# Sixteen experts of a two-layer network: gate/up and down products of fourteen of them as seven quadrant products

## The chip, the cores and the metric

One Trainium2 chip, one of its NeuronCores. The metric is the device time of one execution in microseconds; times of several executions are compared by their median. All arithmetic is float32.

## What is computed

The reference is a network of two layers over 2048 rows of 1024 values. The change touches one part only, the experts at the end of the first layer. Each of 16 experts picks 256 rows (its capacity), and those rows go through a gated feed-forward block with 512 hidden values:

```
def expert_choice_ffn(h, w_router, w_gate, w_up, w_down):
    cap = CAPACITY * N // N_EXPERTS                      # 256 rows
    aff = softmax(h @ w_router)
    gate, idx = top_k(swapaxes(aff, 1, 2), cap)
    xg = h[idx]                                          # 256 x 1024 for each expert
    g = einsum('becd,edf->becf', xg, w_gate)             # 1024 x 512
    u = einsum('becd,edf->becf', xg, w_up)               # 1024 x 512
    y = einsum('becf,efd->becd', silu(g) * u, w_down) * gate
    return zeros_like(h).at[idx].add(y)
```

Everything else (the two mixers, the router, the second layer with its 32 experts) is the same in both kernels.

## The kernel before

The program is a sequence of stages with a barrier between them. The stage `moe1`, the function `experts`, is called once with 16 units. For each expert it does the following.

- SyncE (`sp`) loads the expert's gate, up and down weights (2 MB each) into one of two buffers each. The load of gate and up for expert e+2 waits until the gate/up products of e are made, that of down until its down products are. Behind the last load, `next_columns.load` fills the weight buffer of the next stage's projection (6 MB).
- GpSimd (`pool`) gathers the 256 rows of expert e+2 with two indirect DMAs, and adds the finished rows of e into the target with two more.
- TensorE (`pe`) transposes the gathered rows of the next expert (`turn`, L2981), 16 transposes for each expert in four groups of four, between the gate/up products of this one. Those products (L2999) are four blocks `f` of 128 hidden values; each is 8 matmuls with gate weights and 8 with up weights, a 128x128 weight tile held still and all 256 rows moving. The down products (L3016) are 4 banks of 4 matmuls, 512 output columns moving.
- ScalarE (`act`) copies the transposed rows out with scale and shift (`evacuate`, L3030) and takes Silu of the gate half (L3040).
- VectorE (`dve`) multiplies by the up half (L3057) and, behind the down products, multiplies by the row's gate and the modulation row into `y` (L3070). `gc` (L3054) is a copy of the rows' gates.

In the profile one float32 matmul of the program is two MATMUL records and two LDWEIGHTS records; a transpose is one of each. So an expert's gate/up products are 64 matmuls and 128 records, its down products 16 matmuls and 32 records. PSUM is two banks `psG`, two banks `psT` and four banks `psD`. The experts 0, 1, 14 and 15 are written out; the other twelve run in a loop of six turns.

Of the kernel before, what the change touches and what calls it, by code (L numbers as in the profile page):

```python
# [14 lines left out]
P = 128  # L15
# [2814 lines left out]
def experts(nc, name, K, units, J, FF, x_rows, table, wg, wu, wd, scale2, shift2, n_gates, gate_row, target, block_expert, next_columns,  # L2830
            shared):
# [7 lines left out]
    scatter = block_expert is None  # L2839
    assert FB == 2 * J  # L2840
    WB = 2 if scatter else 4
    TURNS = units // WB
    with Stage(nc, name) as s:
        g_rest = s.sb("g_w", [P, WB - 1, KD, FF])
        u_all = s.sb("u_w", [P, WB, KD, FF])
        g_w = [shared.weights_of(KD, FF)] + [g_rest[:, j, :, :] for j in range(WB - 1)]
        u_w = [u_all[:, j, :, :] for j in range(WB)]
        d_w = s.sb("d_w", [P, WB, FB, D])
        xg = [shared.tile, s.sb("xg", [P, J, D + n_gates])]
        xT = s.sb("xT", [P, 2, KD, N])  # L2850
        sg = s.sb("sg", [P, 2, N])
# [6 lines left out]
        psG = s.ps("psG", [P, 2, BANK])  # L2858
        psT = s.ps("psT", [P, 2, BANK])
        psD = s.ps("psD", [P, 4, BANK])  # L2860
        up_landed = [s.sem(f"up_landed{j}") for j in range(WB)]
        down_landed = [s.sem(f"down_landed{j}") for j in range(WB)]
# [3 lines left out]
        names = ("fixed", "at_ready", "at_out_ready", "gc_ready", "turned", "xT_ready", "made", "silued", "mixed",  # L2866
                 "lowered", "y_ready", "passed")
        (fixed, at_ready, at_out_ready, gc_ready, turned, xT_ready, made, silued, mixed,
         lowered, y_ready, passed) = (s.sem(n) for n in names)
        block = s.block()  # L2870
        STORES = 16 * (J if scatter else 1)
        halves_behind = ((), (0,), (1,), (2, 3))

        def half(i, j):

            return i * (WB // 2) + j // 2

        def turns(engine, body):

            for j in range(WB):  # L2880
                body(0, j, 2)
            with engine.Fori(1, TURNS - 1) as i:
                for j in range(WB):
                    body(i, j, 2)
            for j in range(WB):
                body(TURNS - 1, j, min(2, WB - 1 - j))

        def after(i, j, n):

            return (i, j + n) if j + n < WB else (i + 1, j + n - WB)  # L2890

        def early(i, j):

            return isinstance(i, int) and i == 0 and j < 2

        @block.sync
        def _(sp):
            def load(i, j, first):
                u = i * WB + j
                if scatter:  # L2900
                    e = u
                else:
                    e = sp.value_load(block_expert[0:1, bass.ds(u, 1)], min_val=0, max_val=wg.shape[0] - 1)
                if not first:
                    sp.wait_ge(made, (u - WB + 1) * FB)
                if first and j == 0:
                    sp.sem_inc(up_landed[j], 16)
                    for half, landed in enumerate((first_up, up_landed[j])):
                        c = slice(half * FF // 2, (half + 1) * FF // 2)
                        sp.dma_start(u_w[j][:, :, c], wu[bass.ds(e, 1), :, c].rearrange("e (k p) n -> p (e k) n", p=P)).then_inc(landed, 16)  # L2910
                else:
                    for buf, src in ((g_w, wg), (u_w, wu)):
                        sp.dma_start(buf[j], src[bass.ds(e, 1), :, :].rearrange("e (k p) n -> p (e k) n", p=P)).then_inc(up_landed[j], 16)
                if not first:
                    sp.wait_ge(lowered, (u - WB + 1) * 2 * J)
                sp.dma_start(d_w[:, j, :, :], wd[bass.ds(e, 1), :, :].rearrange("e (k p) n -> p (e k) n", p=P)
                             ).then_inc(down_landed[j], 16)
            for j in range(WB):
                load(0, j, True)
                if scatter and j == 0:  # L2920
                    sp.dma_start(gr[:, :], gate_row.to_broadcast([P, D])).then_inc(fixed, 16)
            with sp.Fori(1, TURNS) as i:
                for j in range(WB):
                    load(i, j, False)
            next_columns.load(sp)

        @block.gpsimd
        def _(pool):
            def gather(i, j):
                u, p = i * WB + j, j % 2  # L2930
                if not early(i, j):
                    pool.wait_ge(turned, (u - 1) * 2 * J)
                    if scatter:
                        pool.wait_ge(gc_ready, u - 1)
                pool.tensor_copy(at[:, p, :], table[:, bass.ds(u * J, J)]).then_inc(at_ready, 1)
                pool.wait_ge(at_ready, u)
# [6 lines left out]
            def put(i, j, left):  # L2943
                u, p = i * WB + j, j % 2
                if left == 2:
                    gather(*after(i, j, 2))
                if isinstance(u, int) and u == units - 1:
                    pool.drain()
# [22 lines left out]
        def _(pe):  # L2971
# [47 lines left out]
            for q in range(2 * J):  # L3019
                turn(0, 0, q)  # L3020
# [1710 lines left out]
```

## Time and profile before

| | |
|---|---|
| median of three executions | 4035.1 us (4034.43 to 4043.13) |
| profiled execution, its own time | 4038.21 us |
| its span | 4036.6 us |
| TensorE busy in the span | 3738.4 us (93%) |
| VectorE busy in the span | 2042.0 us (51%) |
| the experts' stage, first to last instruction | about 1554 to 2262 us |
| one expert in the middle of it | 43.5 us |

In all rows times are microseconds from the start of the span, unless they are marked ns or are a mean in ns. TensorE has two lines: PE for its matmuls, PEld for its weight loads, which run beside the matmuls. A busy time is a union: records that overlap count once. "Idle before" is the engine's idle time ahead of a group, with what ended it. PEclk is the granted TensorE clock as a share of full speed.

### The profile page before, as it was taken

Reading aid. Unit: us, or ns where it says so; the run is one execution under the profiler, and the core shown is the slowest. Engines: PE = TensorE matmul, PEld = TensorE weight load, DVE = VectorE, ACT = ScalarE, POOL = GpSimd, SP = SyncE. Lnnn points to the kernel's source line nnn. Section 1 sums busy time; section 2 is a strip of 40 time slices with the busy share of each in tenths; the row PEclk is TensorE's granted clock in tenths of the full one; section 3 lists DMA queues with packets and bytes.
Section 4 is the critical chain, followed back from the end, with each engine's and each line's share of the span. In section 5 each row is a group of like instructions: output and inputs, shape, how many; then the busy total and the mean of one; then the engine's idle time right before and its main releaser. Section 6 shows DMA issues by size and latency. Waiting matters only on the chain. (4 is left out here: it accounts for less than half of the span.)

```text
span 4036.6 us, 62344 instructions
## 1 busy us (share of the span) xinstructions
PE 3738.4 (93%) x21710; PEld 2426.7 (60%) x21728; DVE 2042.0 (51%) x4259; ACT 1538.0 (38%) x3417; POOL 645.8 (16%) x802
## 2 busy tenths in 40 slices
PE   6999999799898978999999799997999999599998
PEld 4667766555584435777777577774666655344444
DVE  1334343566597763111111278776333466678886
ACT  1122211355563422111111266764333223267775
POOL 0000000100173321111111001011000032322222
PEclk8999999899999988999999899998999999699999
DMA  6222112222435578556556212115222044498974
GB/s 242 78 77 83 71 68 88 88 72 82 129 112 192 182 258 311 183 185 210 187 177 211 70 48 63 59 54 149 68 67 77 23 141 141 167 330 271 333 240 102
DMA packets 227174, 574.09 MB, mean 142 GB/s; under 512 B 28154, under 2 KB 100986, under 8 KB 211118
## 3 DMA queue, kind: packets, MB, share of 16 engines
q1 hardware_dynamic: 177742, 395.92, 28.0%
q0 software_dynamic: 49248, 175.79, 14.9%
q8 instruction: 106, 1.74, 0.2%
q14 instruction: 78, 0.64, 0.1%
HBM read 433.59 MB, written 137.93 MB: 142 GB/s over the span
## 5 line engine op out<-in xcount | busy, mean ns | idle before, releaser
L884 PE MATMUL inp_psU<-inp_w,inp_hT 128*128 128x512 f32 (+3 forms) x1376 | 420.8, 464 | 0.0
L884 PEld LDWEIGHTS inp_psU<-inp_w,inp_hT 128*128 128x128 f32 x1376 | 256.1, 190 | 152.6 <-issue 122.4
L4519 DVE COPY moe_bu<-moe_wu 128x1024 f32 x480 | 299.0, 698 | 38.5 <-issue 19.5
L4406 PE MATMUL moe_psU<-moe_bu,shared_weights 128*32 128x256 f32 x3840 | 295.0, 382 | 1.9 <-issue 1.9
L4406 PE MATMUL moe_psU<-moe_wu,shared_weights 128*32 x1280 | 293.0, 382 | 1.4 <-DVE moe_bu L4519 1.0
L880 PE MATMUL inp_psU<-inp_hT,inp_w 128*128 128x256 f32 x1088 | 244.2, 385 | 9.4 <-DVE inp_tm L686 4.5
L3057 DVE TENSOR_TENSOR moe_hT<-moe_sg,moe_psG 128x256 f32<-128x256 f32 x64 | 27.0, 421 | 438.4 <-ACT moe_sg L3040 438.4
L3040 ACT ACTIVATE moe_sg<-moe_psG 128x256 f32<-128x256 f32 x64 | 24.5, 383 | 568.0 <-PE moe_psG L2999 568.0
L3735 PE MATMUL inp_psU<-shared_weights,inp_w 128*128 128x256 f32 x1024 | 232.3, 382 | 2.9 <-DMA inp_wg<-in_lru_wx 2.9
L880 PEld LDWEIGHTS inp_psU<-inp_hT,inp_w 128*128 128x128 f32 x1088 | 208.0, 193 | 41.5 <-issue 3.9
L2999 PE MATMUL moe_psG<-moe_xT,moe_u_w 128*128 128x256 f32 x1024 | 231.5, 379 | 0.0
L3016 PE MATMUL moe_psD<-moe_d_w,moe_hT 128*128 128x512 f32 x512 | 223.9, 595 | 3.3 <-DVE moe_hT L3057 2.3
L3735 PEld LDWEIGHTS inp_psU<-shared_weights,inp_w 128*128 128x128 f32 x1024 | 195.3, 192 | 36.0 <-issue 10.3
L2999 PEld LDWEIGHTS moe_psG<-moe_xT,moe_u_w 128*128 128x128 f32 x1024 | 194.6, 190 | 26.4
L4475 ACT ACTIVATE moe_bd<-moe_wd 128x1024 f32 x200 | 198.1, 1048 | 29.0 <-PE moe_psD L4428 29.0
L686 DVE COPY inp_tm<-inp_psU 128x512 f32<-128x512 f32 (+3 forms) x86 | 45.4, 527 | 316.0 <-PE inp_psU L884 316.0
L4406 PEld LDWEIGHTS moe_psU<-moe_wu,shared_weights 128*32 128x32 f32 x1280 | 134.2, 110 | 110.9 <-issue 11.2
L3016 PEld LDWEIGHTS moe_psD<-moe_d_w,moe_hT 128*128 128x128 f32 x512 | 96.0, 190 | 122.0 <-issue 119.8
L1317 DVE TENSOR_SCALAR_CACHE_REDUCE att_junk<-att_psS,att_snk 128x640 f32<-128x640 f32 x128 | 108.1, 882 | 108.6 <-PE att_psS L1236 108.6
L4428 PE MATMUL moe_psD<-moe_bd,moe_hT 128*32 128x512 f32 x960 | 153.0, 595 | 0.0
L4406 PEld LDWEIGHTS moe_psU<-moe_bu,shared_weights 128*32 128x32 f32 x3840 | 150.8, 110 | 2.9 <-issue 2.9
L4428 PE MATMUL moe_psD<-moe_wd,moe_hT 128*32 x320 | 151.1, 595 | 1.1 <-ACT moe_hT L4472 0.5
(737 smaller groups left out, 7336.2 us busy)
## 6 DMA issues: line engine op xcount, KB each, us to landing
moe_wu<-in_w_up SPq DMA_DIRECT2D x32, 2048.0 KB, 8.9
moe_d_w<-in_w_down SPq DMA_DIRECT2D x16, 2048.0 KB, 10.6
moe_wd<-in_w_down SPq DMA_DIRECT2D x32, 1024.0 KB, 10.8
moe_u_w<-in_w_up SPq DMA_DIRECT2D x15, 2048.0 KB, 13.4
mod_w<-in_w_ada SPq DMA_DIRECT2D x24, 1024.0 KB, 11.6
inp_mod_w<-in_w_mod SPq DMA_DIRECT2D x16, 1024.0 KB, 5.0
xn<-out_xn POOLq DMA_DIRECT2D x32, 512.0 KB, 4.8
shared_weights<-in_w_gate SPq DMA_DIRECT2D x8, 2048.0 KB, 8.5
```

The lines of the kernel that those rows point to most:

```text
L686: dve.tensor_copy(tm[:, j, at:at + n], psU[:, u % NB, 0:n]).then_inc(tm_kept, by)
L880: mm = pe.matmul(psU[:, u % NB, 0:G], w[:, k, fm_lo + u * P:fm_lo + (u + 1) * P], hT[:, par, k, :], start=(k == 0), stop=(k == KD - 1))
L884: mm = pe.matmul(psU[:, u % NB, 0:n], hT[:, par, k, j * P:(j + 1) * P], w[:, k, lo:lo + n], start=(k == 0), stop=(k == KD - 1))
L1317: dve.tensor_scalar(junk[:, kv, :], psS[:, kv, LO:LO + KEYS], 1.0, snk[:, 1, h:h + 1], ALU.mult, ALU.min, accum_out=low[:, j, h:h + 1]).th ...
L2999: mm = pe.matmul(psG[:, f % 2, at_col:at_col + N], w[j][:, k, f * P:(f + 1) * P], xT[:, p, k, :], start=(k == 0), stop=(k == KD - 1))
L3016: mm = pe.matmul(psD[:, b, :], hT[:, f, r * P:(r + 1) * P], d_w[:, j, f, h * BANK:(h + 1) * BANK], start=(f == 0), stop=(f == FB - 1))
L3057: dve.tensor_tensor(hT[:, f, :], sg[:, f % 2, :], psG[:, f % 2, N:2 * N], ALU.mult).then_inc(mixed, 1)
L3735: mm = pe.matmul(psU[:, m % 2, u % 2 * G:(u % 2 + 1) * G], w[:, k, TM2_W + u * P:TM2_W + (u + 1) * P], hT[:, par, k, :], start=(k == 0), s ...
L4406: mm = pe.matmul(psU[c, f, 0:2 * P], xT[:, p, k, c], w, start=(k == 0), stop=(k == KD - 1), tile_position=(0, g * LOT))
L4428: mm = pe.matmul(psD[c, n, :], hT[:, f, c], w, start=(f == 0), stop=(f == FB - 1), tile_position=(0, g * LOT))
L4475: return act.activation(bd[:, g - 1, f, :].unsqueeze(1), wd[:, bass.ds(slot, 1), f, :], ACT.Copy)
L4519: ins = dve.tensor_copy(bu[:, g - 1, f, c, :].rearrange("p k n -> p (k n)").unsqueeze(1), wu[:, bass.ds(slots[g - 1], 1), f, c, :].rearran ...
```

## The change

Gate and up of an expert are taken as one matrix of two by two quadrants (gate or up; first or second half of the 1024 inputs), the gathered rows as another (input half; first or second 128 rows). The product of two such matrices has eight quadrant products; the new `up` makes seven, on sums of quadrants (`ws1`, `ws2`, `ws4` and `up_of(e, 0)` overwritten on the weights' side; `xt1`, `xt2` and two quadrants of `xT` overwritten on the rows' side), and VectorE joins them with seven additions. `down` does the same with `hT` (`hs1`, `hs2`, `hs4`) and the down weights (`dt1`, `dt2`). A quadrant product of `up` is 16 matmuls with 128 rows moving, one of `down` is 2 matmuls with 512 columns moving. Each product has one of six PSUM banks in turn; `room` waits until the bank's last reader is through. Products run in the order P1, P2, P6, P5, P3, P7, P4. P1 is copied out by ScalarE (`keep`).

The experts 0 and 15 stay as they were (`plain_up`, `plain_down`). The sums, the joined results `U` and `V` and one gate buffer lie in `next_columns.w`, the next projection's weight buffer, whose load now waits until all products of expert 14 are made. The loops are gone: all 16 experts are written out. `make_w_left(e, n)` makes sum n of the weights' side (n = 1, 2, 4: a quadrant sum of 128 x 2048 into `ws1`, `ws2`, `ws4`; n = 3 overwrites `up_of(e, 0)`), `make_x_right` and `make_d_right` likewise on 128 x 512 and 128 x 1024; only the first branch of one of them is shown. Lines with "+" are new.

```
+        lent = next_columns.w[:, :, :].rearrange("p k n -> p (k n)")
+        taken_of_lent = [0]
+        def borrow(a, n):
+            lo = taken_of_lent[0]
+            taken_of_lent[0] = lo + a * n
+            return lent[:, lo:lo + a * n].rearrange("p (a n) -> p a n", a=a)
+        ws1, ws2, ws4 = (borrow(KH, FF) for _ in range(3))
+        xt1, xt2 = (borrow(KH, P) for _ in range(2))
+        dt1, dt2 = (borrow(FH, BANK) for _ in range(2))
+        hs1, hs2, hs4 = (borrow(FH, P) for _ in range(3))
+        U, V, sg_second = (borrow(1, BANK)[:, 0, :] for _ in range(3))
+        gates = [sg[:, :], sg_second]
+        ps = s.ps("ps", [P, BANKS, BANK])
-        psD = s.ps("psD", [P, 4, BANK])
...
+                    if e >= 2:
+                        sp.wait_ge(made, base(e - 2) + (FB if plain(e - 2) else 7))
+                    for buf, src in ((g_w[j], wg), (u_w[:, j, :, :], wu)):
+                        sp.dma_start(buf, src[e:e + 1, :, :].rearrange("e (k p) n -> p (e k) n", p=P)).then_inc(up_landed[j], 16)
+                if e >= 2:
+                    sp.wait_ge(made, base(e - 1))
+                sp.dma_start(d_w[:, j, :, :], wd[e:e + 1, :, :].rearrange("e (k p) n -> p (e k) n", p=P)).then_inc(down_landed[j], 16)
...
+            sp.wait_ge(made, base(LAST))
...
+            def room(n):
+                if n >= BANKS:
+                    reader, count = readers[n - BANKS]
+                    pe.wait_ge(joined if reader == "joined" else kept, count)
...
+            def up_product(e, i, w, x):
+                n = base(e) + i
+                room(n)
+                for f in range(FB):
+                    for k in range(KH):
+                        mm = pe.matmul(bank(n)[:, f * P:(f + 1) * P], w[:, k, f * P:(f + 1) * P], x[:, k, :],
+                                       start=(k == 0), stop=(k == KH - 1))
+                mm.then_inc(made, 1)
+            def up(e):
+                pe.wait_ge(up_landed[e % 2], 32 * (e // 2 + 1))
+                pe.wait_ge(xT_ready, 4 * e + 4)
+                up_product(e, P1, gate_of(e, 0), x_of(e, 0, 0))
+                up_product(e, P2, gate_of(e, 1), x_of(e, 1, 0))
+                turn(e + 1, 0)
+                pe.wait_ge(w_left, 4 * (e - 1) + 2)
+                pe.wait_ge(x_right, 4 * (e - 1) + 2)
+                up_product(e, P6, ws2, xt2)
+                turn(e + 1, 1)
+                up_product(e, P5, ws1, xt1)
+                turn(e + 1, 2)
+                pe.wait_ge(w_left, 4 * (e - 1) + 3)
+                up_product(e, P3, ws4, x_of(e, 1, 1))
+                turn(e + 1, 3)
+                pe.wait_ge(w_left, 4 * (e - 1) + 4)
+                pe.wait_ge(x_right, 4 * (e - 1) + 3)
+                up_product(e, P7, up_of(e, 0), x_of(e, 0, 1))
+                pe.wait_ge(x_right, 4 * (e - 1) + 4)
+                up_product(e, P4, up_of(e, 1), x_of(e, 1, 0))
+            def down_product(e, i, h, w):
+                n = base(e) + 7 + i
+                room(n)
+                for f in range(FH):
+                    mm = pe.matmul(bank(n), h[:, f, :], w[:, f, :], start=(f == 0), stop=(f == FH - 1))
+                mm.then_inc(made, 1)
+            def down(e):
+                pe.wait_ge(down_landed[e % 2], 16 * (e // 2 + 1))
+                pe.wait_ge(mixed, 2 * (e - 1) + 1)
+                down_product(e, P1, h_of(0, 1), d_of(e, 0, 0))
+                down_product(e, P2, h_of(1, 1), d_of(e, 1, 0))
+                pe.wait_ge(h_left, 4 * (e - 1) + 2)
+                pe.wait_ge(d_right, 4 * (e - 1) + 2)
+                down_product(e, P6, hs2, dt2)
+                down_product(e, P5, hs1, dt1)
+                pe.wait_ge(h_left, 4 * (e - 1) + 3)
+                down_product(e, P3, hs4, d_of(e, 1, 1))
+                pe.wait_ge(h_left, 4 * (e - 1) + 4)
+                pe.wait_ge(d_right, 4 * (e - 1) + 3)
+                down_product(e, P7, h_of(0, 0), d_of(e, 0, 1))
+                pe.wait_ge(d_right, 4 * (e - 1) + 4)
+                down_product(e, P4, h_of(1, 0), d_of(e, 1, 0))
+            for e in range(1, LAST):
+                up(e)
+                down(e)
+            plain_up(LAST)
+            plain_down(LAST)
...
+            def silu(e, n):
+                act.wait_ge(joined, joined_by(e, P3 if n else P2))
+                act.activation(gates[n], gates[n], ACT.Silu).then_inc(silued, 1)
+            def keep(e, down, to):
+                act.wait_ge(made, made_by(e, P1, down))
+                act.activation(to, bank(made_by(e, P1, down) - 1), ACT.Copy).then_inc(kept, 1)
+            for e in range(1, LAST):
+                if e > 1:
+                    act.wait_ge(mixed, 2 * (e - 1))
+                keep(e, False, U)
+                silu(e, 0)
+                for q in range(3):
+                    evacuate(e + 1, q)
+                silu(e, 1)
+                evacuate(e + 1, 3)
+                all_stored(act, e - 2)
+                keep(e, True, y_of(e, 0, 0))
...
+            def make_w_left(e, n):
+                if n == 1:
+                    dve.wait_ge(up_landed[e % 2], 32 * (e // 2 + 1))
+                    if e > 1:
+                        dve.wait_ge(made, made_by(e - 1, P5))
+                    ins = dve.tensor_tensor(ws1, up_of(e, 0), up_of(e, 1), ALU.add)
...
+            def make_h_left(e):
+                at_e = 4 * (e - 1)
+                dve.wait_ge(mixed, 2 * e)
+                dve.tensor_tensor(hs1, h_of(0, 0), h_of(1, 0), ALU.add).then_inc(h_left, 1)
+                dve.wait_ge(h_left, at_e + 1)
+                dve.tensor_tensor(hs2, hs1, h_of(0, 1), ALU.subtract).then_inc(h_left, 1)
+                dve.wait_ge(h_left, at_e + 2)
+                dve.tensor_tensor(hs4, h_of(1, 1), hs2, ALU.subtract).then_inc(h_left, 1)
+                dve.wait_ge(h_left, at_e + 3)
+                dve.tensor_tensor(h_of(0, 0), h_of(0, 1), h_of(0, 0), ALU.subtract).then_inc(h_left, 1)
+            def join(e, i, down, to, other, n):
+                dve.wait_ge(made, made_by(e, i, down))
+                if n:
+                    dve.wait_ge(joined, base(e) + 7 * down + n)
+                else:
+                    dve.wait_ge(kept, 2 * (e - 1) + down + 1)
+                dve.tensor_tensor(to, bank(made_by(e, i, down) - 1), other, ALU.add).then_inc(joined, 1)
+            def mix(e, r, up):
+                dve.wait_ge(silued, silued_before(e) + (2 if r else 1))
+                dve.wait_ge(joined, joined_by(e, P4) if r == 0 else joined_by(e, P7) - 1)
+                dve.tensor_tensor(hT[:, :, r * P:(r + 1) * P], tiles(gates[r]), tiles(up), ALU.mult).then_inc(mixed, 1)
+            def weigh(e, r):
+                dve.wait_ge(joined, joined_by(e, P4 if r == 0 else P3, True))
+                dve.scalar_tensor_tensor(out=y[:, e % 2, r, :], in0=y[:, e % 2, r, :], scalar=gc[:, e % 2, r:r + 1],
+                                         in1=gr[:, :], op0=ALU.mult, op1=ALU.mult).then_inc(y_ready, 1)
+            mix_plain(0)
+            make_w_left(1, 1)
+            make_w_left(1, 2)
+            make_x_right(1, 1)
+            make_x_right(1, 2)
+            weigh_plain(0)
+            make_w_left(1, 4)
+            make_w_left(1, 3)
+            make_x_right(1, 3)
+            for e in range(1, LAST):
+                keep_gates(e)
+                make_d_right(e, 1)
+                make_d_right(e, 2)
+                join(e, P2, False, gates[0], U, 0)
+                make_x_right(e, 4)
+                make_d_right(e, 3)
+                join(e, P6, False, U, U, 1)
+                join(e, P5, False, V, U, 2)
+                make_w_left(e + 1, 1)
+                join(e, P3, False, gates[1], V, 3)
+                make_w_left(e + 1, 2)
+                join(e, P7, False, V, V, 4)
+                join(e, P7, False, U, U, 5)
+                mix(e, 1, V)
+                make_x_right(e + 1, 1)
+                make_x_right(e + 1, 2)
+                join(e, P4, False, U, U, 6)
+                mix(e, 0, U)
+                make_h_left(e)
+                make_w_left(e + 1, 4)
+                all_stored(dve, e - 2)
+                join(e, P2, True, y_of(e, 1, 0), y_of(e, 0, 0), 0)
+                join(e, P6, True, y_of(e, 0, 0), y_of(e, 0, 0), 1)
+                make_d_right(e, 4)
+                join(e, P5, True, y_of(e, 0, 1), y_of(e, 0, 0), 2)
+                join(e, P3, True, y_of(e, 1, 1), y_of(e, 0, 1), 3)
+                weigh(e, 1)
+                join(e, P7, True, y_of(e, 0, 1), y_of(e, 0, 1), 4)
+                join(e, P7, True, y_of(e, 0, 0), y_of(e, 0, 0), 5)
+                join(e, P4, True, y_of(e, 0, 0), y_of(e, 0, 0), 6)
+                weigh(e, 0)
+                make_w_left(e + 1, 3)
+                make_x_right(e + 1, 3)
```

## Rows read from the trace of the kernel before

**Rows 1.** Busy time by stretch in the experts' stage, engine by engine, records as x.

```profile
core 0: us, PE busy (x) PEld busy (x) DVE busy (x) ACT busy (x) POOL busy (x), PEclk, DMA share, GB/s
1560.00:1610.00 50.00, 49.05 (x192) 36.71 (x193) 4.77 (x9) 8.19 (x23) 7.66 (x10) 0.95 0.94 339
...
1750.00:1850.00 100.00, 99.64 (x418) 75.43 (x417) 10.37 (x20) 18.65 (x50) 11.13 (x12) 1.00 0.52 168
```

**Rows 2.** Timeline, 1740 to 1790 us: start, duration, instruction, idle before.

```profile
1740.59 3.62 PE L2999 MATMUL moe_psG<-moe_xT,moe_u_w 128*128 128x256 f32 x16
...
1744.05 3.62 PE L2999 MATMUL moe_psG<-moe_xT,shared_weights 128*128 128x256 f32 x16
...
1766.91 14.00 PE L3016 MATMUL moe_psD<-moe_d_w,moe_hT 128*128 128x512 f32 x32 [0.23 <-DVE moe_hT L3057]
...
1780.74 3.62 PE L2999 MATMUL moe_psG<-moe_xT,moe_g_w 128*128 128x256 f32 x16
...
1780.94 0.75 DVE L3070 SCALAR_TENSOR_TENSOR moe_y<-moe_psD,moe_gc,moe_gr 128x512 f32<-128x512 f32 x1 [2.68 <-PE moe_psD L3016]
```

**Rows 3.** Timeline, 1795 to 1835 us.

```profile
1809.25 1.04 PE L2981 MATMUL moe_psT<-ident,shared_rows 128*128 128x128 f32 x8
...
1810.42 14.00 PE L3016 MATMUL moe_psD<-moe_d_w,moe_hT 128*128 128x512 f32 x32
...
1824.25 3.62 PE L2999 MATMUL moe_psG<-moe_xT,shared_weights 128*128 128x256 f32 x16
```

**Rows 4.** Timeline of TensorE in a later attention stage, 2930 to 2950 us.

```profile
2931.01 1.06 PE L3977 MATMUL lata_psO<-lata_v,lata_pT 128*128 128x128 f32 x8
2931.90 0.60 PE L3962 MATMUL lata_psP<-ident,lata_p_long 128*128 128x128 f32 x4
2932.34 1.06 PE L3977 MATMUL lata_psO<-lata_v,lata_pT 128*128 128x128 f32 x8
```

**Rows 5.** Groups by line and shape: TensorE, 128x128 and ahead of it the loads.

```profile
L3977 PE MATMUL lata_psO<-lata_v,lata_pT 128*128 128x128 f32 x544 | 74.6, 278 | 5.9 <-ACT lata_pT L4062 3.0 <-DVE lata_o L4023 2.9
...
L3977 PEld LDWEIGHTS lata_psO<-lata_v,lata_pT 128*128 128x128 f32 x544 | 67.9, 194 | 6.8 <-DVE lata_o L4023 3.4 <-issue 3.4
```

**Rows 6.** Groups by line and shape: VectorE.

```profile
L3070 DVE SCALAR_TENSOR_TENSOR moe_y<-moe_psD,moe_gc,moe_gr 128x512 f32<-128x512 f32 x64 | 48.1, 751 | 190.9 <-PE moe_psD L3016 190.9
...
L2214 DVE TENSOR_TENSOR out_xo<-out_psO,out_part 128x512 f32<-128x512 f32 x56 | 38.6, 689 | 75.3 <-PE out_psO L2393 62.2 <-DMA xn<-out_xn 12.3 <-DVE out_part L2242 0.5
...
L3351 DVE TENSOR_TENSOR inp_nope<-inp_qs,inp_hs 128x256 f32<-128x256 f32 x32 | 13.5, 422 | 1.3
...
L3388 DVE TENSOR_TENSOR inp_ig<-inp_ig,inp_xc 128x1024 f32<-128x1024 f32 x8 | 9.8, 1225 | 0.6
...
L2191 DVE TENSOR_TENSOR out_w<-out_w,shared_rows 128x2048 f32<-128x2048 f32 x2 | 4.5, 2288 | 3.0 <-DMA out_w<-in_w_out 3.0
```

**Rows 7.** One line of VectorE with its shortest, median and longest instruction (ns).

```profile
L2165 DVE TENSOR_TENSOR out_xo<-out_xo,out_x x14: 1224/1226/2068, 3267.6 to 3448.6; 128x1024 f32<-128x1024 f32 x14
```

**Rows 8.** Timeline, 1410 to 1425 us.

```profile
1410.69 0.69 DVE L2214 TENSOR_TENSOR out_xo<-out_psO,out_part 128x512 f32<-128x512 f32 x1 [1.78 <-PE out_psO L2393]
...
1411.41 1.39 DVE L2165 TENSOR_TENSOR out_xo<-out_xo,shared_rows 128x1024 f32<-128x1024 f32 x1
1411.80 2.15 POOL L2507 TENSOR_TENSOR out_left<-out_mixT,out_left 128x512 f32<-128x512 f32 x1
```

**Rows 9.** Groups by line and shape in the experts' stage: GpSimd.

```profile
L2961 POOL DMA_INDIRECT x<-moe_y,moe_at_out x32 | 51.0, 1595 | 590.6 <-DVE moe_y L3070 549.1 <-DVE moe_gc L3054 41.5
L2939 POOL DMA_INDIRECT moe_xg<-xn,moe_at x16 | 15.7, 982 | 9.1 <-POOL moe_at L2935 6.7 <-issue 2.4
```

**Rows 10.** DMA issues in the experts' stage: count, KB each, median us to landing.

```profile
moe_d_w<-in_w_down SPq DMA_DIRECT2D x16, 2048.0 KB, 10.6
moe_u_w<-in_w_up SPq DMA_DIRECT2D x15, 2048.0 KB, 13.4
...
inp_w<-in_w_in SPq DMA_DIRECT2D x2, 896.0 KB, 22.3
```

More of the change, by code:

```diff
@@ L2865, in experts @@
         stored = [s.sem(f"stored{j}") for j in range(2)]
[L2866 to L2869, printed above, removed]
+        names = ("fixed", "at_ready", "at_out_ready", "gc_ready", "turned", "xT_ready", "made", "silued", "joined", "kept", "mixed",
+                 "w_left", "x_right", "h_left", "d_right", "y_ready", "passed")
@@ L2870, in experts @@
+        (fixed, at_ready, at_out_ready, gc_ready, turned, xT_ready, made, silued, joined, kept, mixed,
+         w_left, x_right, h_left, d_right, y_ready, passed) = (s.sem(n) for n in names)
         block = s.block()
[L2871 to L2894, printed above, removed]
+        def silued_before(e):
+            return 0 if e == 0 else 4 + 2 * (e - 1)
+        def x_of(e, depth, r):
+            return xT[:, e % 2, depth * KH:(depth + 1) * KH, r * P:(r + 1) * P]
+        def h_of(depth, r):
+            return hT[:, depth * FH:(depth + 1) * FH, r * P:(r + 1) * P]
+        def d_of(e, depth, h):
+            return d_w[:, e % 2, depth * FH:(depth + 1) * FH, h * BANK:(h + 1) * BANK]
@@ L2896, in _ @@
         @block.sync
         def _(sp):
[L2898 to L2901, printed above, removed]
-                else:
[L2903 to L2917, printed above, removed]
@@ L2928, in _, with gather @@
         def _(pool):
[L2929 to L2936, printed above, removed]
+            def gather(e):
+                p = e % 2
+                if e >= 2:
+                    pool.wait_ge(turned, (e - 1) * 4)
+                    pool.wait_ge(gc_ready, e - 1)
+                pool.tensor_copy(at[:, p, :], table[:, e * J:(e + 1) * J]).then_inc(at_ready, 1)
+                pool.wait_ge(at_ready, e)
                 pool.sem_inc(passed, 1)
@@ L2964, in _ @@
             pool.wait_ge(first_up, 16)
-            gather(0, 1)
-            turns(pool, put)
+            gather(1)
+            for e in range(units):
+                put(e)
             for p in range(2):
@@ L2971, in _, with turn @@
         def _(pe):
-            def turn(i, j, q):
-                u, p = i * WB + j, j % 2
+            def turn(e, q):
+                if e > LAST:
+                    return
                 r, h = divmod(q, 2)
                 if q == 0:
-                    pe.wait_ge(gathered[p], half(i, j) * 16 * J + 16 * J)
-                if not (early(i, j) and j == 0 and r == 0):
-                    pe.wait_ge(xT_ready, u * 2 * J + q - 1)
+                    pe.wait_ge(gathered[e % 2], STORES * (e // 2 + 1))
+                if 4 * e + q >= 2:
+                    pe.wait_ge(xT_ready, 4 * e + q - 1)
@@ L3019, in _ @@
-            for q in range(2 * J):
-                turn(0, 0, q)
-            turns(pe, body)
+                        n = base(e) + FB + 2 * r + h
+                        room(n)
+                        for f in range(FB):
+                            mm = pe.matmul(bank(n), hT[:, f, r * P:(r + 1) * P], d_w[:, e % 2, f, h * BANK:(h + 1) * BANK],
+                                           start=(f == 0), stop=(f == FB - 1))
+                        mm.then_inc(made, 1)
[7 more added lines that the diff above has]
+                mm.then_inc(made, 1)
@@ L3036, in body @@
                 for f in range(FB):
-                    act.wait_ge(made, u * FB + f + 1)
-                    if not (early(i, j) and j == 0 and f < 2):
-                        act.wait_ge(mixed, u * FB + f - 1)
-                    act.activation(sg[:, f % 2, :], psG[:, f % 2, 0:N], ACT.Silu).then_inc(silued, 1)
-                    if left:
-                        for q in halves_behind[f]:
-                            evacuate(*after(i, j, 1), q)
-            for q in range(2 * J):
-                evacuate(0, 0, q)
@@ L3069, in body @@
[L3069 to L3075 removed]
+                        n = base(e) + FB + 2 * r + h
```

275 lines of the change are left out of this document (180 added, 95 removed).

## The prediction

> **What bounds the kernel now.** I read the busy time by stretch first. In the middle of the experts' stage TensorE is busy 99.64 of 100 us at full clock, VectorE 10.4, ScalarE 18.7, and the DMA engines about half [rows 1]. So the stage lasts as long as TensorE's queue, and only fewer or cheaper matmul records shorten it. The timelines give their price. Sixteen records of 256 columns run from 1740.59 to 1744.05, 216 ns each [rows 2]. The 14.00 us of a down block are 32 records of 512 columns, the last of which lasts about 0.6 us, so a step is 429 ns. Eight transposes and the turn to the down block take 1.17 us [rows 3]; I price 16 of them at 1.76 us, 110 ns each. One expert lasts from 1780.74 to 1824.25, 43.51 us [rows 2, 3]: 128 x 0.216 = 27.65, 32 x 0.429 = 13.73, 1.76, and 0.37 of small waits at the turns between the blocks.
>
> **TensorE's part of the change.** Each of 14 experts goes from 128 records of 256 columns to 7 x 16 matmuls, 224 records of 128 columns. The stage has no such stream, only transposes. The nearest is in a later attention stage, also float32, 128x128 weights, 128 columns, two records for each matmul: eight records and the start of the next group take 0.89 us, and those eight with four transposes go from 2931.01 to 2932.34, 1.33 us for twelve [rows 4]: 111 ns a step. That is the price I take. The group's row says 74.6 us for 544, or 137 ns [rows 5], but a union of runs of eight counts each run's last record in full (1.06 us for a step of 0.89) and the next group's start again. It is the upper bound. The lower bound is half of 216, 108 ns.
> Gate/up: 224 x 0.111 = 24.86 us in place of 27.65, so an eighth fewer columns saves a tenth. Down: 7 products of 4 records, 28 x 0.429 = 12.01 in place of 13.73. Transposes stay. The new expert is 24.86 + 12.01 + 1.76 = 38.63 us in place of 43.51, of which the 0.37 of turns vanishes only if no wait stands there. Saved: 4.88 us x 14 = 68 us.
>
> A rule speaks against this. The LDWEIGHTS of 128 columns last 194 ns each by the profile and overlap with the matmuls and one another, since the steps are 111 ns [rows 4, 5]. The Trainium skill (TensorE: Matmul & The Clock Gate, section Back-to-back issue gap) says that load and matmul together set the spacing, 81 ns at 128 columns where the formula for the isolated matmul gives 56; by that ratio of 1.45 the step here would be an estimated 155 ns and the expert 48.5 us. The trace's 111 ns decides against it, in runs of 12 records only.
>
> **VectorE's part.** It has 4 sums of 128x2048 at 2.29 us, 4 of 128x1024 at 1.225, 4 of 128x512 (xT) at 0.69, 4 of 128x256 at 0.42, 14 joins and 2 mixes of 512 at 0.69 [rows 6], 2 weighings of 1024 in SBUF (no row; between the 0.75 of 512 and twice that, so 1.27 by the growth of the sums), one copy of the gates at 0.16. That is 9.2 + 4.9 + 2.8 + 1.7 + 11.0 + 2.5 + 0.2 = 32.3, and 35 gaps of 0.03 [rows 8] make 33.4 us of 38.6. It fits, but the queue is in order, so I lay it beside TensorE's from t = 0 at the first up product (3.55 us a product, 0.44 four transposes, 1.72 a down product; results reach VectorE 0.20 us after the next matmul's start, 1780.94 against 1780.74 [rows 2], and I take the same back).
> Up P6 starts at 7.54, P5 at 11.5, P3 at 15.5, P7 at 19.5, P4 at 23.06; down starts at 26.6, its P6 at 30.0, P4 at 36.9.
> - P7's result is seen at 23.26. Two joins, mix, and two xT sums of the next expert end at 26.9; P4's result has just come (26.8). Join, mix, `hs1`, `hs2` end at 29.25, so TensorE may go at 29.45 where it needs them at 30.0. This is the tightest place, 0.6 us, and its cover is the two down products on rows whose mix is done (needed at 26.6, there at 25.4).
> - `hs4`, the h quadrant, `ws4` of the next expert, three joins and the last d sum end about 35.2, before 36.9.
> - Behind down P4 VectorE has a tail: joins to 40.1, weighing 41.4, weights and xT quadrants to 44.5, that is 5.9 us into the next expert, two d sums 8.4, then P2's join (made at 7.1). P7 wants those quadrants at 19.5. It has caught up by P6 at 11.3.
> - Banks: a product needs the reader of the sixth before it. The closest is down P7, needing up P4's join (27.6) at 35.2. Free.
> - ScalarE: about 8 us an expert before [rows 1] and two copies of 512 more. The evacuation that the third group of transposes needs at 15.1 stands behind P2's join (9) and one Silu; there is room.
> So I put a stall of 0.3 us an expert in the sum, 4 us in all, for the tight place; 0 is the lower bound.
>
> **Moved and removed.** The load of gate and up for e+2 is issued at 26.6 of e, and u lands 13.4 us later [rows 10], at 1.4 of e+1; VectorE first reads it at 15.3. Down weights issued at a start land at 10.6, read at 5.9 of the next. On SyncE's queue nothing else stands between them. Bytes: three weights of 2 MB, 1 MB gathered and 1 MB added, 8.4 MB an expert over 38.6 us, are 217 GB/s, under the 339 of the stage's first stretch [rows 1]. GpSimd keeps two gathers and two scatters; the gather for e+1 goes out some 7 us into e-1, so about 30 us early. The projection's 6 MB go out at the start of expert 15; they landed in at most 22.3 us [rows 10], under its 43 us. If that cover were gone it would cost those 22 us once. Expert 1's sums: its up weights are to be there before the sums are wanted at about 1593, since all 8.5 MB issued ahead fit in 25 to 30 us at 339 GB/s; VectorE then runs 0.5 us later than in steady state. Loops gone: the written-out experts 0 and 1 lie in the first stretch, where TensorE is busy 49.05 of 50 us with the DMA engines at 0.94 [rows 1], so written-out code costs nothing there, and the loop cost nothing to be gained.
>
> **The sum.** 4038.2 (the profiled execution) - 68 + 4 = 3974. The median is 3.1 us lower, 4035.1, so 3971.
>
> **Rivals.**
> - VectorE falls late, 20 in 100. For: 33.4 of 38.6 us with 0.6 us of room at one place; the two-input sum of 1024 has lasted 1.39 and up to 2.07 us, not 1.226, beside GpSimd's work [rows 7, 8]. GpSimd has two scatters and two gathers of 1.6 and 0.98 us an expert [rows 9], 5.2 us with 0.9 us of copies on top; if each held VectorE up, it would need 39.5 us, and as the queue is in order TensorE would wait 1 to 2.5 us an expert. Against: the scatters and gathers fall between 38 and 8 of the next, where there is slack. Time: 3967 + 14 to 35, 3981 to 4002.
>  The Trainium skill (SBUF — State Buffer, section Who interferes with whom) says that a tensor_tensor with both inputs in SBUF contends with GpSimd's reads and the later one blocks wholly; the 1.39 and 2.07 us agree, and whether an indirect DMA counts as such a read no row shows.
> - The 128-column step is 137 ns in trains of 32 (the group's row), slower, 5 in 100: 224 x 0.137 = 30.7, expert 44.5, 1.0 us x 14 more, 4049. It decides from a step of (43.51 - 13.77)/224 = 133 ns. Against: no idle is seen between the runs that give 111.
> - Loads don't overlap, 2 in 100: 224 x 0.194 = 43.5, expert 57.2, 13.7 x 14 more, 4227. The page's rule above goes this way, a third as far. The rows of 111 ns exclude nearly all of it.
> - Weights, instructions of the written-out code, or the projection's load come late, 4 in 100: some 20 to 50 us lost, 3990 to 4020.
> That the change doesn't make fewer columns is excluded; it is in the code.
>
> **Numbers.** Forecast 3971, 69 in 100, its own range 3962 to 3980. Half the time of the first rival is under 3992, so 3960 to 3994 holds about 8 in 10. A change of 0.2% (8 us) is about what can be told from none. Faster: 69 + 20 + 3 = 92; within 0.2%: 2; slower: 6.
>
> **What would show it.** In the changed profile: the up matmuls at 111 ns a step in trains of 32, 38.6 to 39 us an expert, VectorE about 85 busy of 100 us, TensorE over 97, and the first matmul of down P6 waiting 0 to 0.5 us on `hs2`. Wrong, if the step is 130 or more, if waits on `joined`, `w_left` or `x_right` stand before up P6 or P7, or if the next stage waits for its weights.

## The result, and the profile after

The changed kernel takes 3973.05 us (median of 4, 3966.75 to 3976.59), the kernel before in the same session 4039.11 (4034.43 to 4043.72): a ratio of 0.9835, interval 0.9815 to 0.9854. Beside each other once more on another chip they took 3968.44 and 4033.32, ratio 0.9837 [0.9823, 0.985]. Forecast were 3971 and a range of 3960 to 3994.

Busy time by stretch of the changed kernel; the two rows answer to [rows 1]:

```profile
1560.00:1610.00 50.00, 47.16 (x184) 35.46 (x184) 9.07 (x11) 13.13 (x36) 6.01 (x8) 0.87 0.92 338
1750.00:1850.00 100.00, 100.00 (x660) 79.91 (x659) 82.05 (x94) 19.07 (x47) 19.11 (x14) 1.00 0.68 219
```

TensorE doesn't idle in the middle of the stage. VectorE has gone from 10.37 to 82.05, the DMA engines from 168 to 219 GB/s, and neither stops it. The timeline from 1755 to 1800 us shows one whole expert, from down block to down block:

```profile
1756.13 3.60 PE L3092 MATMUL moe_ps<-moe_d_w,moe_hT 128*128 128x512 f32 x8
...
1758.31 0.42 DVE L3260 TENSOR_TENSOR inp_w<-inp_w,moe_hT 128x256 f32<-128x256 f32 x1
...
1759.57 3.60 PE L3092 MATMUL moe_ps<-inp_w 128*128 128x512 f32 x8
...
1767.94 1.61 POOL L2996 DMA_INDIRECT x<-moe_y,moe_at_out  x1 [27.47 <-DVE moe_y L3283]
...
1770.54 2.28 DVE L3210 TENSOR_TENSOR moe_u_w<-moe_g_w,moe_u_w 128x2048 f32<-128x2048 f32 x1
1771.46 2.82 POOL L2996 DMA_INDIRECT x<-moe_y,moe_at_out  x1 [1.91 <-DVE moe_y L3283]
...
1775.73 3.74 PE L3063 MATMUL moe_ps<-inp_w 128*128 128x128 f32 x32
...
1777.00 1.22 DVE L3249 TENSOR_TENSOR moe_d_w<-moe_d_w 128x1024 f32<-128x1024 f32 x1
...
1777.08 1.97 POOL L2974 DMA_INDIRECT moe_xg<-xn,moe_at  x1 [0.30 <-issue]
...
1779.30 0.60 PE L3018 MATMUL moe_psT<-ident,shared_rows 128*128 128x128 f32 x4
...
1783.51 0.69 DVE L3273 TENSOR_TENSOR inp_w<-moe_ps,inp_w 128x512 f32<-128x512 f32 x1 [3.32 <-PE moe_ps L3063]
...
1794.91 3.60 PE L3092 MATMUL moe_ps<-moe_d_w,moe_hT 128*128 128x512 f32 x8
1795.10 0.37 SPq L2954 DMA_DIRECT2D moe_g_w<-in_w_gate  x1
1795.11 0.69 DVE L3273 TENSOR_TENSOR inp_w<-moe_ps,inp_w 128x512 f32<-128x512 f32 x1 [0.16 <-PE moe_ps L3063]
```

- From 1756.13 to 1794.91 are 38.78 us, against 43.51 [rows 2, 3]: 4.73 us saved in each of 14 experts, 66.2 in all.
- A product of 32 records of 128 columns goes from 1775.73 to the transposes at 1779.30: 3.57 us, 111.6 ns a record in a long train, where [rows 4] gave 111 from trains of 12.
- `hs2` ends at 1758.73 and down P6, which reads it, starts at 1759.57 with no idle time in brackets: 0.84 us lie between them in the tight place.
- VectorE waits for TensorE, 3.32 us ahead of P5's join and 0.16 ahead of P4's.

The whole stage I measure from its first transpose to the first row load of the next stage. In before:

```profile
1553.93 1.94 PE L2981 MATMUL moe_psT<-ident,shared_rows 128*128 128x128 f32 x8 [6.86 <-PEq L76]
...
2268.01 0.82 SPq L3198 DMA_DIRECT2D shared_rows<-x  x2
```

and after:

```profile
1559.55 1.94 PE L3018 MATMUL moe_psT<-ident,shared_rows 128*128 128x128 f32 x8 [6.92 <-PEq L76]
...
2207.61 0.81 SPq L3454 DMA_DIRECT2D shared_rows<-x  x2
```

That is 714.1 and 648.1 us: 66.0 less, all of the gain and the 66.2 of the experts. Below, "the stage" is this measure. The spans differ by 62.0 only: this profile reached the stage 5.6 us later and was 1.6 us shorter behind it. The next projection's first matmul waits 2.47 us for a small load (`inp_wg`), so the 6 MB of its weights cost nothing.

### The profile page after: what moved, and what is told of

It reads as the page before. It is cut to its first block and busy times, and to the rows that moved or that the text cites. A ratio compares the mean times of both kernels' runs of the same rounds, so it can differ in the third digit from the quotient of the medians.

```text
span 3974.6 us, 65105 instructions
## 1 busy us (share of the span) xinstructions
PE 3673.2 (92%) x22998; PEld 2426.7 (61%) x23016; DVE 2407.5 (61%) x4623; ACT 1549.3 (39%) x3417; POOL 686.1 (17%) x802
## 5 line engine op out<-in xcount | busy, mean ns | idle before, releaser
L2996 POOL DMA_INDIRECT x<-moe_y,moe_at_out x32 | 68.3, 2136 | 482.0 <-DVE moe_y L3283 414.8
L1363 ACT ACTIVATE att_p<-att_psS,att_low 128x640 f32<-128x640 f32 x128 | 101.2, 792 | 119.3 <-DVE att_junk L1317 97.9
L4714 ACT ACTIVATE shared_weights<-moe_psT,mod_cols,mod_scale 128x128 f32<-128x128 f32 x320 | 120.1, 457 | 48.6 <-PE moe_psT L4650 48.6
L4318 ACT ACTIVATE lata_pT<-lata_psP 128x512 f32<-128x512 f32 (+3 forms) x112 | 61.1, 549 | 159.4 <-PE lata_psP L4218 159.4
L3129 ACT ACTIVATE moe_xT<-moe_psT,mod_cols,mod_scale 128x128 f32<-128x128 f32 x256 | 95.4, 456 | 70.7 <-PE moe_psT L3018 70.6
L3273 DVE TENSOR_TENSOR inp_w<-moe_ps,inp_w 128x512 f32<-128x512 f32 x84 | 58.1, 692 | 104.0 <-PE moe_ps L3063 102.6
```

The source lines that it names most:

```text
L1363: act.activation(p[:, g % 2, kv, :], psS[:, kv, LO:LO + KEYS], ACT.Exp, scale=-1.0, bias=low[:, j, h:h + 1], accum_out=sums[:, j, h:h + 1] ...
L2996: pool.indirect_dma_start(out=target, out_offset=bass.IndirectOffsetOnAxis(ap=at_out[:, p, r:r + 1], axis=0), in_=y[:, p, r, :], in_offset ...
L3129: ins = act.activation(xT[:, e % 2, k, r * P:(r + 1) * P], psT[:, h, (k % 4) * P:(k % 4 + 1) * P], ACT.Identity, scale=scale2[k], bias=shi ...
L4714: ins = act.activation(xT[:, p, k, :], psT[:, q, (k % 4) * P:(k % 4 + 1) * P], ACT.Identity, scale=scale2[k], bias=shift2[k])
```

## The experiments

The versions are made from the changed kernel, with two sets, `UP7` and `DOWN7`, that say which experts make their gate/up and their down products in seven. Ratios are to the kernel before, run on the same chip.

**The same program with nothing in seven products.** It keeps six PSUM banks, written-out experts and the later projection load.

```
-    def plain(e):
-        return e in (0, LAST)
+    UP7, DOWN7 = set(range(0)), set(range(0))
```

> All 16 experts make their products as before (64 and 16 matmuls), in the rewritten program: no loops, six PSUM banks in turn, load of the next projection's weights at the start of the last expert. Theory A (the gain is TensorE's fewer records alone): the time of the kernel before, 4039 us within 5, one expert 43.5 us, the stage from its first transpose to the next stage's first load 714 us. Theory B (a part of the gain comes from the rewrite: loops, banks, waits at the turn between blocks): 10 to 25 us below the kernel before, one expert 42 to 43 us.

Measured: 4035.16 against 4035.66, ratio 1.000 [0.9991, 1.001]; stage 713.0 us, an expert 43.44. So loops, banks and the place of the load are worth nothing, as predicted, and the whole gain is in the products.

**Each half alone.**

```
+    UP7, DOWN7 = set(range(1, 15)), set(range(0))  # up_only
+    UP7, DOWN7 = set(range(0)), set(range(1, 15))  # down_only
```

> Experts 1 to 14 make gate/up in seven quadrant products, down as before in 16 matmuls. Theory A: gate/up is 224 steps of 0.1116 us in place of 128 of 0.216, 25.0 in place of 27.65 us, so 2.65 us an expert and up to 0.37 more where the wait at the turn to the down products goes: 37 to 42 us below the kernel before, about 4000. Theory C (128-column products are worth nothing, the whole gain lies in the down products and the turns): within 5 us of the kernel before, one expert 43.5 us.

> Experts 1 to 14 make down in seven quadrant products, gate/up as before in 64 matmuls. Theory A: 28 steps of 0.429 us in place of 32, 1.72 us an expert, 24 us below the kernel before, about 4015; with the run of gate/up alone the two savings add up to the 66 us of both. Theory C: the whole 66 us less, about 3973.

TensorE's timeline, first with gate/up alone, then with down alone:

```profile
1757.95 13.90 PE L3093 MATMUL moe_ps<-moe_d_w,moe_hT 128*128 128x512 f32 x32
1771.69 7.31 PE L3102 MATMUL moe_ps<-moe_xT,moe_g_w 128*128 128x128 f32 x64
...
1798.44 13.90 PE L3093 MATMUL moe_ps<-moe_d_w,moe_hT 128*128 128x512 f32 x32
```

```profile
1766.08 3.67 PE L3134 MATMUL moe_ps<-moe_d_w,moe_hT 128*128 128x512 f32 x8
...
1778.17 3.62 PE L3076 MATMUL moe_ps<-moe_xT,moe_g_w 128*128 128x256 f32 x16
...
1807.82 3.67 PE L3134 MATMUL moe_ps<-moe_d_w,moe_hT 128*128 128x512 f32 x8
```

Gate/up alone: 3992.08, ratio 0.9892 [0.9876, 0.9909]; an expert takes 40.49 us, 3.02 less than [rows 2, 3], which is 27.65 - 25.00 = 2.65 and the 0.37 of waits at the turns. Down alone: 4010.87, ratio 0.9935 [0.9918, 0.9951]; an expert takes 41.74, 1.77 less (13.73 - 12.01 = 1.72). Together that is 4.79 us an expert beside 4.73 for both in one. The medians save 43.6 (37 to 42 were expected) and 24.8 us, together 68.4, beside 66.1. They add up but for 2 us, which is within what the rest of the program varies by (below); TensorE never waits for what either adds.

**How much room VectorE has, and where.** Two needless 128x1024 sums, 2.47 us an expert, are put in a place where VectorE waits anyway, and then into the tight chain.

```
                     join(e, P6, False, U, U, 1)
+                    (two sums)                      # extra_slack
                     join(e, P5, False, V, U, 2)
...
                     join(e, P7, False, U, U, 5)
+                    (the same two sums)             # extra_tight
                     mix(e, 1, V)
```

> The changed kernel with one of VectorE's sums (128x1024, 1.22 us) made twice more for each of 14 experts, in the place where VectorE has idled 3.3 us, between the joins of up products P6 and P5. Theory A (only the stretch from P7's result to the second h sum can hold TensorE up): no change, 3973 us within 5, one expert 38.8 us. Theory D (VectorE as a whole is at its limit, 82 of 100 us busy, and anything more falls on TensorE): 2.5 us an expert, 34 us more, about 4007.

> The same two extra sums (2 x 1.22 us) placed between the joins of up product P7 and the first mix. Theory A: in the changed kernel the second h sum ends 0.84 us before the first matmul that reads it, of which about 0.2 is the way between the engines; so of 2.5 us more some 1.9 fall on TensorE, one expert 40.7 us, 26 us more, about 3999. Theory D: the same 34 us as in the other place. Theory E (the room is larger than it looks, since the end of P4's join and not P7's starts the chain): under 10 us more.

The stretch from 1750 to 1850 us with the sums in the slack, then in the tight chain:

```profile
1750.00:1850.00 100.00, 100.00 (x660) 79.91 (x660) 87.95 (x101) 18.74 (x45) 23.04 (x17) 1.00 0.72 234
```

```profile
1750.00:1850.00 100.00, 96.49 (x617) 75.08 (x616) 83.80 (x97) 17.43 (x42) 16.76 (x13) 1.00 0.65 211
```

In the slack they cost nothing: 3969.66, ratio 0.9839 [0.9823, 0.9856], stage 647.5, with VectorE the busier for it. In the chain: 3987.95, ratio 0.9891 [0.9874, 0.9907], stage 670.3, so 18.3 us by the medians and 22.9 by the stage where 26 were expected. The timeline of the latter shows which waits:

```profile
1796.63 3.67 PE L3135 MATMUL moe_ps<-moe_d_w,moe_hT 128*128 128x512 f32 x8 [1.17 <-issue]
...
1799.75 0.42 DVE L3310 TENSOR_TENSOR inp_w<-inp_w,moe_hT 128x256 f32<-128x256 f32 x1
...
1800.23 3.70 PE L3135 MATMUL moe_ps<-inp_w 128*128 128x512 f32 x8
```

From the first gate/up product (1768.54) to down P1 are 28.09 us, where the changed kernel has 26.76 (1768.15 to 1794.91). So P1 comes 1.33 us late on the mixed rows (the 1.17 in brackets counts from the modelled end of the record before), and that place had 2.47 - 1.33 = 1.1 us of room (predicted 1.2). P6 follows it after 3.60 us where 3.43 is its pace, 0.17 late: `hs2` has just ended at 1800.17. The product behind it is 0.10 late too. The expert takes 40.37 us (1756.26 to 1796.63) in place of 38.78, and 14 x 1.6 = 22 us are nearly the 22.9 of the stage. That the medians differ by less goes with the rest of the program, which was 5.6 us shorter behind the stage in this profile than in that of extra_slack. Room in one place of an in-order queue is not room in another, and VectorE's busy share tells of neither.

**One expert more, and all of them.** Expert 15 too has its sums in the projection's buffer, so the first half of that load goes out once its gate/up products are made, the rest after the last down product. The second version adds expert 0.

```
+    UP7, DOWN7 = set(range(1, 16)), set(range(1, 16))    # fifteen
+    UP7, DOWN7 = set(range(16)), set(range(16))          # sixteen
-            sp.wait_ge(made, base(LAST))
-            next_columns.load(sp)
+            sp.wait_ge(made, base(LAST) + ups(LAST))
+            (columns of k 0 to 3)
+            sp.wait_ge(made, base(LAST) + ups(LAST) + 7)
+            (columns of k 4 to 7)
```

> Experts 1 to 15 in seven products each, so the next projection's weight buffer is in use to the end of the stage: the first half of its rows is loaded behind expert 15's up products, the second half behind its last down product. Theory A (the next stage needs about 21 us from the last down product to its first matmul with these weights, and 3 MB land in under 14): 4.7 us less than the changed kernel for the expert, 1.3 us back for VectorE's longer tail, so 3970. Theory F (the load is exposed): the first projection matmul waits for the weights, 5 to 15 us more than the changed kernel.

> All 16 experts in seven products each; expert 0's sums are made as soon as its up weights have landed. Theory A: another 4.7 us less than with fifteen, 3965, if the sums of expert 0 (two of 2.3 and two of 0.69 us behind a landing about 1 us after TensorE may start) are there 7.5 us after its start. Theory F: the first expert waits for them, up to 3 us given back at the start, beside what the late load costs.

Measured: fifteen 3964.70, ratio 0.9826 [0.9809, 0.9842], stage 647.5; sixteen 3968.74, ratio 0.9841 [0.9824, 0.9857], stage 645.9. Expected were 3970 and 3965. An expert more should have taken 4.7 less 1.3, so 3.4 us, off the stage and took 0.5. From expert 15's first up product to the end of its last down product are 37.2 us in fifteen and 42.7 in the changed kernel, so 5.5 are saved there, and 0.6 more by a faster start of expert 0. What is lost lies behind. The end of the stage in the changed kernel and in fifteen (lines of GpSimd, then of TensorE):

```profile
2200.23 1.55 POOL L2996 DMA_INDIRECT x<-moe_y,moe_at_out  x1 [5.33 <-DVE moe_y L3186]
2207.61 3.55 POOL L4021 MEMSET inp_fm<- 128x4144 f32 x1 [5.83 <-POOLq L76]
```

```profile
2214.81 1.97 PE L3907 MATMUL inp_psT<-ident,shared_rows 128*128 128x128 f32 x8 [16.18 <-DVE shared_rows L3502]
```

```profile
2191.53 1.55 POOL L3032 DMA_INDIRECT x<-moe_y,moe_at_out  x1 [1.98 <-DVE moe_y L3332]
2203.15 3.55 POOL L4085 MEMSET inp_fm<- 128x4144 f32 x1 [10.07 <-POOLq L76]
```

```profile
2210.40 1.97 PE L3971 MATMUL inp_psT<-ident,shared_rows 128*128 128x128 f32 x8 [21.80 <-DVE shared_rows L3566]
```

GpSimd waits 10.07 us for its last row addition to land, where it waits 5.83 in the changed kernel, and TensorE idles 21.80 us at the change of stage where it idles 16.18: 5.6 us given back. Of these 4.2 are the later landing, since the barrier waits for it; the load of 3 MB issued at 2188.62, ahead of the last row addition at 2191.53, is the suspect. The remaining 1.4 are VectorE's longer tail: the last row addition starts 2.9 us after the last product ends, 1.6 in the changed kernel.

In sixteen, expert 0 takes 44.4 us by seven products against 46.5 by eight in the changed kernel (46.0 in fifteen):

```profile
1561.90 10.34 PE L3102 MATMUL moe_ps<-moe_xT,shared_weights 128*128 128x128 f32 x64 [1.77 <-ACT moe_xT L3170]
1572.74 0.66 PE L3054 MATMUL moe_psT<-ident,moe_xg 128*128 128x128 f32 x4 [0.50 <-DMA moe_xg<-xn,moe_at]
...
1593.99 3.67 PE L3134 MATMUL moe_ps<-moe_d_w,moe_hT 128*128 128x512 f32 x8 [1.42 <-issue]
```

Its first 64 records take 10.34 us where 7.31 is the pace at full clock; but by eight products the first 16 records cost as much more at the lower clock, 6.55 us for 3.45 in the changed kernel. What is lost beyond that are waits of its own: the gathered rows come 0.50 us late and the mixed rows 1.42 late, since VectorE stood 5.09 us for expert 1's up weights. Expert 0 was worth 1.6 to 2.1 us, not 4.7. Sixteen's median is nonetheless 4 us above fifteen's; its profile is 3.2 us longer behind the stage, where the code is the same.

**The projection load out of the last rows' way.** Expert 15's sums move to expert 14's spent gathered rows and to the other half of `xT`, so all of the load goes out before the last rows do.

```
+        last_dt = shared.tile[:, :, :].rearrange("p r c -> p (r c)")
+        last_hs = xT[:, 0, :, :].rearrange("p k n -> p (k n)")
...
-            sp.wait_ge(made, base(LAST) + ups(LAST))
+            sp.wait_ge(made, made_by(LAST, P3))
...
-            sp.wait_ge(made, base(LAST) + ups(LAST) + 7)
+            sp.wait_ge(mixed, 2 * nU(units))
```

> Experts 1 to 15 by seven products, as in fifteen, but expert 15's sums lie in expert 14's spent gathered rows and in the other half of its own transposed rows, so that the projection load goes out during expert 15: the first third once its up product P3 is made, the rest once its mixes are done. Theory A (in fifteen the last scatter landed late beside the 3 MB load, which gave back about 5.6 us): the idle time of TensorE at the change of stage falls from 21.8 us to 16 to 17.5, the stage takes 643 to 645 us against fifteen's 647.5, and the time is 2 to 5 us under fifteen's. Rival F (the loads cost the down products or the last rows the same wherever they lie): the stage stays at 647 to 648 us and the time equals fifteen's within 1.5 us.

> All 16 experts by seven products, with the placement of fifteen_early for expert 15 and that of sixteen for expert 0. Theory A: the stage takes about 641 to 643 us, some 4 less than sixteen's 645.9 and 1.6 to 2 less than fifteen_early's, since expert 0 takes 44.4 us by seven products against 46.5 by eight. Rival F: 645 to 646 us, the same as sixteen.

```profile
2187.02 1.55 POOL L3043 DMA_INDIRECT x<-moe_y,moe_at_out  x1 [1.98 <-DVE moe_y L3345]
2194.43 3.55 POOL L4098 MEMSET inp_fm<- 128x4144 f32 x1 [5.86 <-POOLq L76]
```

```profile
2201.56 1.97 PE L3984 MATMUL inp_psT<-ident,shared_rows 128*128 128x128 f32 x8 [17.47 <-DVE shared_rows L3579]
```

GpSimd's wait is back at 5.86 us, and TensorE idles 17.47, the 16.18 of the changed kernel and 1.3 for the tail. The stage takes 642.5: 5.1 less than in fifteen, 4.2 by the rows that land earlier and the rest because expert 0, with the same code, took 45.1 us in place of 46.0. So the load beside the last rows was the cause of those 4.2. Under the down products it costs nothing: expert 15 takes 37.2 us as in fifteen. The times are 3959.74, ratio 0.9812 [0.9799, 0.9825], for fifteen_early and 3964.36, ratio 0.981 [0.9796, 0.9823], for sixteen_early, whose stage takes 641.5. The ratios don't tell the two apart, and the 1.0 us between their stages is no more than expert 0's start varies by.

**The better version beside the changed kernel.** Both ran unaltered on one chip, in one session.

> The changed kernel itself, unchanged, on one chip beside the version with experts 1 to 15 by seven products and the early projection load. Its ratio to before should be 0.983 to 0.985, its stage 648 us from the first transpose to the next stage's first row load.

> By the stage's own times (642.5 us against 648.1) this version should be 4 to 7 us faster than the changed kernel when both run on one chip, a ratio of 0.9815 to 0.983 to before. Rival: the gain in the stage is given back in the stages behind it, and the two medians agree within 2 us.

Measured: 3968.44 (3965.0 to 3970.4) and 3959.76 (3957.31 to 3964.49), ratios 0.9837 [0.9823, 0.985] and 0.982 [0.9806, 0.9833]. The version with 15 experts is 8.7 us faster than the changed kernel, more than the 4 to 7 expected. Its stage is 5.1 us shorter (643.0 against 648.1). Its profile reached the stage 2.9 us later and is 6.6 us shorter behind it, which makes the 8.7 of the spans. From the next stage's row load to the end of the span are 1767.0 and 1766.0 us in the two profiles of the changed kernel, 1759.0 and 1759.4 in the two of this version, whose code there is the same. Most of that lead comes about in the later attention stage. Busy time over the whole of it, for the changed kernel and then for this one:

```profile
2719.90:3136.60 416.70, 402.42 (x2272) 271.24 (x2272) 156.51 (x309) 136.94 (x241) 34.71 (x64) 0.98 0.24 69
```

```profile
2715.70:3126.30 410.60, 396.34 (x2272) 266.95 (x2272) 156.49 (x309) 136.91 (x241) 34.70 (x64) 1.00 0.24 70
```

The same 2272 matmul records take 6.1 us longer, at a granted clock of 0.98 in place of 1.00, while VectorE and ScalarE are busy equally long. A clock lower by about 0.02 over 410 us is of that size. Gate/up alone had such a short remainder too (1761.9), and so had extra_tight (1761.1) with the changed kernel's 14 experts, while sixteen_early had not (1766.4), so it doesn't go with the number of experts. What sets the clock there stays open. Over all profiles the remainder lies between 1759.0 and 1768.6 us, so medians that differ by a few us say nothing here of a single step; the stage's own time does.

## Why the prediction held, point by point

- **TensorE's part** was the whole answer. Its sum is 224 x 0.1116 + 28 x 0.429 + 4 x 0.435 = 38.75 us, and 38.78 was measured; the sum of the prediction was 38.63. The step of 111 ns, taken from trains of 12 records, held in trains of 64 with the LDWEIGHTS of 190 ns hidden. The Trainium skill (TensorE: Matmul & The Clock Gate, section Back-to-back issue gap) has load and matmul together set the spacing; the 155 ns estimated from it is not what these float32 trains show. The rival with 137 falls as well: that figure was the union's, not the engine's.
- **The stall of 0.3 us an expert** was the wrong term: there is none. The place itself was laid out well: 0.84 us lie between `hs2` and down P6, where the prediction had 0.75 and, less the way back, 0.6. That room was worked out and then a stall put in beside it all the same. The 4 us for it, less the 2.1 by which the steps were priced too low, leave the 2 us between the 64 forecast and the 66 measured: two small errors of opposite sign. The forecast started from 4035.1, while the kernel before took 4039.11 in the result's session, so the saving, 64 against 66, says more than the 2 us between 3971 and 3973.05; that it comes so close is partly luck. The profiled execution was forecast at 3974 and took 3976.59, with 5.6 us of it lost ahead of the stage.
- **VectorE** was forecast at 33.4 us an expert and takes 31.8 (82.05 of 100 us for 38.78). The prices held: the weighing, put at 1.27, lasts 1.285, and the sums are as in [rows 6]. But the gaps of 0.03 that were added are overlaps in many places: the sum at 1770.54 lasts 2.28, and the next instruction starts at 1772.74.
- **The rival in which GpSimd holds VectorE up** (20 in 100) did not come: VectorE's sums of 1024 average 1.22 us, as alone. GpSimd is the one that waits (below), and it has time for it. Only the tiny copy of the gates is lengthened, by 0.25 us, in a place with room. Had VectorE lost 2.5 us in the tight chain, the cost would have been the 22 us of extra_tight.
- **Late weights** did not come. The rows of the DMA issues that answer to [rows 10]:

```profile
moe_d_w<-in_w_down SPq DMA_DIRECT2D x16, 2048.0 KB, 13.2
...
moe_u_w<-in_w_up SPq DMA_DIRECT2D x15, 2048.0 KB, 14.0
```

Both land somewhat later than before, far ahead of their reader. **Loops and written-out code** are worth nothing, shown by all_plain.

## What to carry to other kernels

Where one engine is busy all the time and the others are not, seven products for eight can pay as fully as here, as long as each sum has its place in an in-order queue: lay the queue of the helping engine beside the busy one and look for the shortest room, since the same 2.5 us cost nothing in one place and 22 us in another. Price a new instruction by the distance between the starts of a train of its kind, not by the mean or the union of short runs. And when a load is moved toward a barrier, look at what small transfers must land before that barrier: 3 MB in front of the last rows gave back 4.2 us, nearly what one whole expert saves.

## What the runs showed of the hardware

**GpSimd yields to VectorE's sums.** Groups by line and shape of GpSimd in the experts' stage, after; they answer to [rows 9]:

```profile
L2996 POOL DMA_INDIRECT x<-moe_y,moe_at_out x31 | 66.8, 2155 | 476.7 <-DVE moe_y L3283 414.8 <-DVE moe_y L3186 61.8
L2974 POOL DMA_INDIRECT moe_xg<-xn,moe_at x16 | 24.6, 1534 | 9.1 <-POOL moe_at L2970 6.7 <-issue 2.4
```

Row additions went from 1595 to 2155 ns, gathers from 982 to 1534. With gate/up alone they are 2175 and 985, with down alone 1721 and 985, with all plain 1601 and 982. The timeline above tells when. The addition at 1767.94, beside joins that read PSUM and SBUF, takes 1.61 us. The one at 1771.46 starts inside a sum with both inputs in SBUF, which ends at 1772.82, and takes 2.82: 1.27 longer, about the rest of that sum. The gather at 1777.08 starts 0.08 us after the start of such a sum of 1.22 and takes 1.97 in place of 0.98. The Trainium skill (SBUF — State Buffer, section Who interferes with whom) says that the two contend through a shared read port when VectorE reads both inputs from SBUF and GpSimd reads too, and that the port is an exclusive lock, so that the order of issue decides who blocks. The trace agrees for GpSimd's side.

For VectorE's side it agrees in part. A sum that starts during a row addition keeps its length: the one at 1772.74 lasted its usual 0.69 us, the weighing at 1769.33 its 1.28. The copy of the gates between two such sums doesn't:

```profile
1773.34 0.41 DVE L3169 COPY moe_gc<-moe_xg 128x2 f32<-128x2 f32 x1
```

It takes 0.41 us in each of experts 2 to 14, where it starts during the lengthened row addition, and 0.16 in expert 1 and with gate/up or down alone, where it doesn't. Beside a tensor_tensor of GpSimd's own, in [rows 8], a VectorE sum was lengthened too, 1.39 us for 1.22. Why the sums pass beside a row addition and the copy does not stays open.

**The start of the stage runs at the lower clock.** From 1560 to 1570 us the granted clock is 0.50 of full speed, 1.2 GHz, after TensorE had idled at the turn of the stage:

```profile
1560.00:1570.00 10.00, 7.21 (x23) 5.38 (x23) 0.00 (x0) 5.69 (x16) 2.28 (x5) 0.50 0.93 319
```

The first 16 records of expert 0 take 6.72 us in this profile where the third group takes 3.62. By eight products that costs 1.5 (up_only) to 3.1 us (this profile) over what the full clock would take, by seven 3.0 in sixteen and 2.7 in sixteen_early. So the same code's stage varies by up to 1.6 us with it, and two stage times that differ by less than that tell of nothing; an expert's time in the middle of the stage, at the full clock, is free of it.
